# Two-layer block with a seven-product feed-forward stage: operands of successive pairs in alternating places, made one pair ahead

## What is computed

```python
h = rms_norm(x, norm2_g)
x = x + (silu(h @ w_gate) * (h @ w_up)) @ w_down      # D = 1024, F = 2816
```

## Time and profile before

| What | Value |
|---|---|
| Median of 3 runs (lowest, highest) | 2658.61 us (2657.32, 2658.63) |
| Profiled execution: its own time | 2658.09 us |
| Profiled execution: its span | 2655.9 us |
| TensorE matmul busy | 2608.4 us, 98% of the span |
| VectorE busy | 1566.0 us, 59% |
| ScalarE busy | 1131.5 us, 43% |
| GpSimd busy | 181.7 us, 7% |
| Moved by DMA | 296.76 MB, mean 112 GB/s |
| Mean granted TensorE clock, share of 2.4 GHz | 0.995 |

### The profile page before, as it was taken

One profiled execution on the slowest core, in us unless ns is written; L12 is line 12 of the kernel. 1 busy time (PEld: TensorE's weight loads), 2 busy tenths in 40 slices (PEclk: granted clock), 3 DMA queues, 4 the chain that ended last, 5 costly groups with the idle time before them and its releaser, 6 DMA issues.

```text
span 2655.9 us, 36717 instructions
## 1 busy us (share of the span) xinstructions
PE 2608.4 (98%) x15173; PEld 2181.4 (82%) x15173; DVE 1566.0 (59%) x2427; ACT 1131.5 (43%) x1714; POOL 181.7 (7%) x123
## 2 busy tenths in 40 slices
PE   9999999999999999999999999899999999989998
PEld 5788888988888879888888777798998777788997
DVE  7877767644444456543455666663763566664674
ACT  2343233533333344332343665452553465453453
POOL 0000000000000000000000110120310010020220
PEclk9999999999999999999999999999999999989999
DMA  9345754222222211232232212132233211223222
GB/s 402 129 190 209 283 197 177 90 81 79 80 80 80 75 70 67 109 103 92 94 108 106 77 64 80 64 108 92 96 109 128 82 64 64 79 80 119 80 97 86
DMA packets 46759, 296.76 MB, mean 112 GB/s; under 512 B 5121, under 2 KB 7297, under 8 KB 17410
## 3 DMA queue, kind: packets, MB, share of 16 engines
q1 hardware_dynamic: 46592, 294.42, 30.4%
q10 hardware_dynamic: 2, 0.00, 0.0%
HBM read 292.30 MB, written 2.10 MB: 111 GB/s over the span
## 4 chain that ended last, share of the span: by engine, by line
PE 85%; DVE 5%; ACT 3%; issue 3%; POOL 3%; POOLq 0%; DVEq 0%; ACTq 0%
PE PS L631 84%; POOL QV L2447 3%; ACT QH L1184 1%; PE PS L689 1%; DVE QL L1749 1%; DVE QV L1749 1%; ACT WH L1184 1%; DVE WL L1749 0%; ACT KEPT L1184 0%; DVE TV L1752 0%; DVE XT L1749 0%; DVE TV L1749 0%; DVE AA L1749 0%; DVE SId L1749 0%; POOL SId L2447 0%
## 5 line engine op out<-in xcount | busy, mean ns | idle before, releaser
L1749 DVE TENSOR_TENSOR WL<-RAW,WH 128x1024 fp32r<-128x1024 f32 (+1 forms) x328 | 429.8, 1310 | 443.4 <-ACT WH L1184 441.8
L631 PE MATMUL PS<-H1H,WH 128*128 128x512 f32 (+1 forms) x1568 | 602.6, 384 | 0.7 <-DVE H1L L1749 0.3
L631 PE MATMUL PS<-H1L,WH 128*128 128x512 f32 (+1 forms) x1568 | 590.5, 377 | 0.0
L631 PE MATMUL PS<-H1H,WL 128*128 128x512 f32 (+1 forms) x1568 | 590.4, 377 | 0.0
L1184 ACT ACTIVATE WH<-RAW 128x1024 fp32r<-128x1024 f32 (+1 forms) x328 | 365.4, 1114 | 246.0 <-PE PS L631 215.0
L631 PEld LDWEIGHTS PS<-H1H,WH 128*128 128x128 f32 x1568 | 295.2, 188 | 60.6 <-issue 5.4
L631 PEld LDWEIGHTS PS<-H1L,WH 128*128 128x128 f32 x1568 | 295.2, 188 | 56.2 <-issue 4.1
L631 PEld LDWEIGHTS PS<-H1H,WL 128*128 128x128 f32 x1568 | 295.0, 188 | 54.7
L631 PE MATMUL PS<-TH,QH 128*128 128x256 f32 x1008 | 291.7, 289 | 34.6 <-ACT KEPT L1184 22.7
L631 PE MATMUL PS<-TL,QH 128*128 128x256 f32 x1008 | 287.7, 285 | 0.0
L631 PE MATMUL PS<-TH,QL 128*128 128x256 f32 x1008 | 287.6, 285 | 0.0
(11 more groups left out here) (296 smaller groups left out, 4060.5 us busy)
## 6 DMA issues: line engine op xcount, KB each, us to landing
RAW<-stream SPq DMA_DIRECT2D x169, 1024.0 KB, 4.8
AR<-stream SPq DMA_DIRECT2D x56, 1024.0 KB, 7.2
RAW<-stream SPq DMA_DIRECT2D x64, 704.0 KB, 4.0
RT<-ret SPq DMA_DIRECT2D x2, 1536.0 KB, 6.7
MIX<-stream SPq DMA_DIRECT2D x4, 640.0 KB, 17.0
XT<-xt SPq DMA_DIRECT2D x4, 512.0 KB, 5.6
y<-XT SPq DMA_DIRECT2D x16, 128.0 KB, 1.8
MIX<-stream SPq DMA_DIRECT2D x1, 1024.0 KB, 17.0
```

What stands on the lines that cost most here:

```text
L631: return nc.tensor.matmul(out, weights, moving, start=start, stop=stop, skip_group_check=True)
L1749: return nc.vector.tensor_tensor(out, a, b, op)
```

## The change

- `STD` goes from 4 to 5: each of the two stages has five plain pairs in front, and 17 seven-product pairs instead of 18 (34 in the kernel).
- Operands lie in three places: W (where they were), H (over `H1H` and `H1L`) and G (over the part of `GHd`/`GLd` that the first seven-product pair's own output and later ones use), with a last block of G at 223232. The first pair of a stage has G, then H and W alternate. In a second half the first pair has H.
- `site(s)` replaces `product`: an operand of pair s may be written once the last pair that used the same place is through (for W also the last plain tile, for H the last plain tile in front, for G the tile before the stage).
- All operands of pair s+1 are made during pair s, on VectorE and ScalarE, in a new order. The fourth kept part moves to the head of the next pair's list on ScalarE (`last_kept`).
- The sums S2 and S4 move from GpSimd to VectorE (`second_sum`, `fourth_sum`).
- The homes of plain tiles go round by three throughout; the lists of fixed homes in the two stages are gone.
- The 19 factor steps are spread over five plain pairs.
- Semaphores `qh`, `ql` are called `qhd`, `qld`, since `qh`, `ql`, `qv` are now functions that give a block of a pair's place.

The core of the diff:

```diff
-STD = 4
+STD = 5
@@ homes
-    of, last, fixed = {}, SPLIT % 3 - 1, {}
-    for f0 in (FFN2, FFN3):
-        fixed.update(zip(range(f0 + 22, f0 + 30), (0, 1, 2, 0, 1, 0, 1, 2)))
-        fixed[f0 + 52] = 0
-    fixed.update(zip(range(FFN3, FFN3 + 2 * STD), (2, 0, 1, 2, 1, 0, 1, 2)))
...
+    plain = [t for t in range(SPLIT, NTILE) if not seven(t)]
+    return {t: (SPLIT + n) % 3 for n, t in enumerate(plain)}
+def sites():
+    out = {}
+    for f0 in (FFN2, FFN3):
+        for half in range(2):
+            for jj in range(0 if half else STD, HC):
+                first = jj == STD and not half
+                out[f0 + 30 * half + 2 * jj] = "G" if first else "H" if jj % 2 == 0 else "W"
+    return [out[t] for t in PAIRS]
@@ Core
-        self.QH, self.QL, self.QV = at("QH", 68096, 3584, F32R), at("QL", 84992, 3584, F32R), at("QV", 84992, 3584)
+        self.QH = {x: at("QH" + x, a, 3584, F32R) for x, a in (("W", 68096), ("H", 18432), ("G", 124928))}
+        self.QL = {x: at("QL" + x, a, 3072 if x == "G" else 3584, F32R)
+                   for x, a in (("W", 84992), ("H", 35072), ("G", 149504))}
+        self.QV = {x: at("QV" + x, a, 3072) for x, a in (("W", 84992), ("H", 35072), ("G", 149504))}
+        self.QLG = at("QLGA22", 223232, 512, F32R)
-    def product(self, s, name):
...
+    def site(self, s):
+        t, x = PAIRS[s], SITE[s]
+        f0 = FFN3 if t >= FFN3 else FFN2
+        pairs = [p + 1 for p, y in zip(PAIRS, SITE) if p < t and y == x]
+        if x == "W":
+            pairs.append(max(u for u in HOME if u < t))
+        return self.mm, mm_at(max(pairs[-2:] + [f0 + 2 * STD - 1 if x == "H" else f0 - 1]))
@@ act_program, seven_kept
+        if past:
+            last_kept(f, t - 2)
+        if more:
+            weights_high(s + 1)
         q.wait_ge(c.prod, 5 * s + 1)
         q.wait_ge(c.sa, 22 * (f - 2) + j)
         act(c.KEPT1[:, 0:256], E[:, 256:512]).then_inc(c.kept, 1)
-        if j % HC and seven(t - 2):
+        if past:
             gated_high(f, t0, j - 1)
         q.wait_ge(c.prod, 5 * s + 2)
         q.wait_ge(c.c2, s)
         act(c.KEPT2[:, 256:512], D[:, 256:512], scale=-1.0).then_inc(c.kept, 1)
+        if more:
+            sums_high(s + 1)
         q.wait_ge(c.prod, 5 * s + 3)
         act(c.KEPT1[:, 256:512], E[:, 256:512]).then_inc(c.kept, 1)
         if more:
-            weights_high(s + 1)
-            sums_high(s + 1)
+            second_high(s + 1)
+            rest_high(s + 1)
         else:
             prep(t + 2)
         q.wait_ge(c.sa, 22 * (f - 2) + j + 1)
         act(SI[:, :], SI[:, :], ACT.Silu).then_inc(c.si, 1)
-        if more:
-            second_high(s + 1)
-        q.wait_ge(c.mm, mm_at(t + 1))
-        act(c.KEPT2[:, 0:256], E[:, 256:512]).then_inc(c.kept, 1)
-        if more:
-            rest_high(s + 1)
-        else:
+        if not more:
+            last_kept(f, t)
             prep(t + 3)
             gated_high(f, t0, j)
@@ dve_program, seven_out
-        third_sum(s)
+        if more:
+            first_sum(s + 1)
         if past:
             gated(f, j - 1)
-        rest_low(s)
+        if more:
+            weights_low(s + 1)
+            second_sum(s + 1)
         if past:
             gated_low(f, j - 1)
         if more:
-            first_sum(s + 1)
-            weights_low(s + 1)
+            third_sum(s + 1)
+            fourth_sum(s + 1)
+            sums_low(s + 1)
+            second_low(s + 1)
+            rest_low(s + 1)
         else:
             prep(t + 2)
         q.wait_ge(c.mm, mm_at(t))
...
         tt(SI[:, :], D[:, :], c.KEPT1[:, :], ALU.subtract).then_inc(c.sa, 1)
-        if more:
-            sums_low(s + 1)
-            second_low(s + 1)
-        else:
+        if not more:
@@ dve_program, ffn
-                    factors(f, ((), (4, 5, 6, 7), (10, 11, 12), (15, 16))[jj])
+                    factors(f, ((), (4, 5, 6, 7), (10, 11), (14, 15), (18,))[jj])
...
-                    factors(f, ((0, 1, 2, 3), (8, 9), (13, 14), (17, 18))[jj])
+                    factors(f, ((0, 1, 2, 3), (8, 9), (12, 13), (16, 17), ())[jj])
@@ pool_program
-        for s in range(len(PAIRS) // 2 * l, len(PAIRS) // 2 * (l + 1)):
...
-            tt(c.QV[:, S2:S2 + 512], c.QV[:, S1:S1 + 512], raw[:, 0:512], ALU.add).then_inc(c.sum2, 1)
...
-            tt(c.QV[:, S4:S4 + 512], c.QV[:, S2:S2 + 512], raw[:, 512:1024], ALU.add).then_inc(c.sum4, 1)
```

More of the change, by code:

```diff
@@ L316, in homes @@
 def homes():
-    of, last, fixed = {}, SPLIT % 3 - 1, {}
-    for f0 in (FFN2, FFN3):
-        fixed.update(zip(range(f0 + 22, f0 + 30), (0, 1, 2, 0, 1, 0, 1, 2)))
-        fixed[f0 + 52] = 0
-    fixed.update(zip(range(FFN3, FFN3 + 2 * STD), (2, 0, 1, 2, 1, 0, 1, 2)))
[L323 to L326, removed]
+    plain = [t for t in range(SPLIT, NTILE) if not seven(t)]
+    return {t: (SPLIT + n) % 3 for n, t in enumerate(plain)}
 HOME = homes()
 COUNT = {t: n + 1 for n, t in enumerate(HOME)}
-def before(t, home):
-    return max((u for u in HOME if u < t and HOME[u] == home), default=3)
+def sites():
[6 more added lines that the diff above has]
+    return [out[t] for t in PAIRS]
+SITE = sites()
 BANK = banks()
@@ L503, in __init__ @@
         self.sum1, self.sum2, self.sum3, self.sum4 = (sem(f"sum{i}") for i in (1, 2, 3, 4))
-        self.qh, self.ql, self.prod, self.kept, self.c2 = (sem(n) for n in ("qh", "ql", "prod", "kept", "c2"))
+        self.qhd, self.qld, self.prod, self.kept, self.c2 = (sem(n) for n in ("qhd", "qld", "prod", "kept", "c2"))
     def xk(self, k):
@@ L519, in vacant, with qh, ql, qv @@
     def vacant(self, t):
[L521 to L525, removed]
-    def product(self, s, name):
[L529 to L535, removed]
+        plain = [u for u in HOME if u < t and HOME[u] == HOME[t]]
+        pairs = [p for p, x in zip(PAIRS, SITE) if p < t and x == "W"]
+        return self.mm, mm_at(max(plain[-1:] + [p + 1 for p in pairs[-1:]], default=3))
+    def site(self, s):
[5 more added lines that the diff above has]
+        return self.mm, mm_at(max(pairs[-2:] + [f0 + 2 * STD - 1 if x == "H" else f0 - 1]))
+    def qh(self, s, o, n):
+        return self.QH[SITE[s]][:, o:o + n]
+    def ql(self, s, o, n):
+        return self.QLG[:, o - A22:o - A22 + n] if SITE[s] == "G" and o >= A22 else self.QL[SITE[s]][:, o:o + n]
+    def qv(self, s, o, n):
+        return self.QV[SITE[s]][:, o:o + n]
     def pair(self, s):
@@ L1351, in seven_kept @@
         s, D, E, SI = PAIRS.index(t), PS[BANK[t]], PS[BANK[t + 1]], c.SI[f][j % HC % 2]
-        more = seven(t + 2)
+        more, past = seven(t + 2), j % HC and seven(t - 2)
+        if past:
+            last_kept(f, t - 2)
+        if more:
+            weights_high(s + 1)
         q.wait_ge(c.prod, 5 * s + 1)
@@ L1964, in first_sum, with second_sum, fourth_sum @@
         q.wait_ge(*ready)
-        q.wait_ge(*c.product(s, "S1"))
-        tt(c.QV[:, S1:S1 + 512], raw[:, 1024:1536], raw[:, 1536:2048], ALU.add).then_inc(c.sum1, 1)
+        q.wait_ge(*c.site(s))
+        tt(c.qv(s, S1, 512), raw[:, 1024:1536], raw[:, 1536:2048], ALU.add).then_inc(c.sum1, 1)
+    def second_sum(s):
+        raw = c.pair(s)[1]
+        q.wait_ge(c.sum1, s + 1)
+        tt(c.qv(s, S2, 512), c.qv(s, S1, 512), raw[:, 0:512], ALU.add).then_inc(c.sum2, 1)
+    def fourth_sum(s):
+        raw = c.pair(s)[1]
+        q.wait_ge(c.sum2, s + 1)
+        tt(c.qv(s, S4, 512), c.qv(s, S2, 512), raw[:, 512:1024], ALU.add).then_inc(c.sum4, 1)
@@ L1985, in second_low @@
     def second_low(s):
-        q.wait_ge(c.qh, 4 * s + 3)
-        q.wait_ge(*c.product(s, "A22"))
-        tt(c.QL[:, A22:A22 + 512], c.pair(s)[1][:, 1536:2048], c.QH[:, A22:A22 + 512].bitcast(F32), ALU.subtract
-           ).then_inc(c.ql, 1)
+        q.wait_ge(c.qhd, 4 * s + 3)
+        q.wait_ge(*c.site(s))
+        tt(c.ql(s, A22, 512), c.pair(s)[1][:, 1536:2048], c.qh(s, A22, 512).bitcast(F32), ALU.subtract
+           ).then_inc(c.qld, 1)
     def rest_low(s):
-        q.wait_ge(c.qh, 4 * s + 4)
+        q.wait_ge(c.qhd, 4 * s + 4)
@@ L2113, in ffn @@
                     second_low(follow)
+                    rest_low(follow)
             for n in range({0: 5, 3: 6}.get(f, 8) if half else 8):
@@ L2124, in ffn @@
                     second_low(PAIRS.index(t0 + 30))
+                    rest_low(PAIRS.index(t0 + 30))
                 if not half:
```

63 lines of the change are left out of this document (33 added, 30 removed).

## The result

The changed kernel takes 2618.25 us (median of 4 runs, 2616.72 to 2620.54), the kernel before 2658.56 us on the same chip. The ratio is 0.985, with a 95% interval of 0.9833 to 0.9867: 40.3 us less, where 41.4 were forecast. The profiled execution has a span of 2614.9 us (2655.9 before).

A forecast was written before the change was run, and what follows sets the result against it. TensorE's own pace was taken as the bound, with 34.5 us of waits listed. From 2658.1 us, -23.6 (steady waits) + 1.7 (plain pairs) - 19.5 (entries) gave 2616.7, plus 0.5 for the median: 2617 us, range 2609 to 2629.

The forecast's parts named there:

- The steady loop: Steady pairs: alternating places remove TensorE's wait of 0.66 us for a kept part in 34 waits, 23.6 us gained.
- VectorE's work: Steady pairs: with two sums more, VectorE works 9.2 of 10.06 us, so TensorE still bounds.
- about 9.8 us busy in a pair: Sign of a right forecast: VectorE's busy time in a steady pair of the changed kernel.
- 0.9 us are left: Steady pairs: VectorE's room in a period of 10.06 us, held against VectorE becoming the bound.
- VectorE becomes the bound: Rival, steady pairs: period 10.3 to 10.6 us, returning 8 to 18 us of gain, say 2630 us; chance 0.10.
- Two plain pairs: Two seven-product pairs become plain, 10.9 us each for 10.06: 1.7 us more.
- The entries: First seven-product pairs of both stages: waits shrink from 12.0 and 14.9 us to 3.9 and 3.5, gaining 19.5 us.
- TensorE is 0.4 us later against it: Second stage's entry: TensorE 0.4 us later relative to VectorE than in the first, so 3.5 us lost, not 3.9.
- I take no fall: Entries: the clock stays 1.00 behind spells of 1.35 and 2.5 us; otherwise the sum is 3.4 us higher.
- Loads and second halves: Loads land after 4.8 us, wanted 12.0 us after release; second halves' first kept part is in time: no cost.
- the late load: Rival, steady pairs: loads over 12.0 us hold a kept part, 2685 us at 14 us; chance 0.04.
- a returned wait: Rival, steady pairs: the 0.66 us wait comes back behind another instruction, only entries gain, 2641 us; chance 0.05.

The follow-up runs named there:

- experiment 1: Kernel before, with only the sums S2 and S4 moved from GpSimd to VectorE, one place kept: 2656.16 us, ratio 0.9994.
- experiment 2: Changed kernel with the sums S2 and S4 back on GpSimd: 2624.37 us, ratio 0.9873.
- experiment 5: Changed kernel with one needless 512-column VectorE instruction in each pair: 2622.68 us, ratio 0.9868.
- experiment 6: Changed kernel with two needless 512-column VectorE instructions in each pair, the second waiting for the first: 2644.03 us, ratio 0.9947.
- experiment 7: Changed kernel with one needless VectorE instruction a pair and the last kept part set ahead of SiLU on ScalarE: 2618.39 us, ratio 0.9854.
- experiment 8: Changed kernel, entry reordered: first pair's third and fourth sums, high and low parts before the fifth plain pair's gating, next high weights later: 2620.43 us, ratio 0.9859.
- experiment 10: Changed kernel run again unaltered, on one chip with a repeat of a third entry order: 2619.11 us, ratio 0.9855.
- experiment 3: Changed kernel with four plain pairs instead of five and the weights' factors spread over four: 2627.6 us, ratio 0.9886.
- experiment 4: Kernel before with five plain pairs, factors spread likewise and homes going round by three; one place and GpSimd's sums stay: 2645.15 us, ratio 0.9952.
- experiment 9: Changed kernel with a third entry order: all first-pair operands made before the fifth plain pair's gate, its SiLU and gating moved later: 2613.5 us, ratio 0.9833.
- experiment 11: Changed kernel with the third entry order (first-pair operands before the fifth plain pair's gate), repeated beside the unaltered change on one chip: 2613.99 us, ratio 0.9835.

## Why the prediction was right, and where its steps were off

**The steady loop** (forecast 23.6, measured 23.1). Confirmed by the profile, and by experiments 1 and 2 as a matter of places and not of the engine that makes the sums. The prediction did not separate the two. It took the loop from the chain of GpSimd's sum; experiment 1 shows that the loop closes also without GpSimd, through the low parts at 1895.94. Whoever had read "GpSimd is slow" from the earlier trace rows would have made half the change for nothing.

**VectorE's work** was forecast at 9.2 us a pair and measured at 9.10 busy. The line "about 9.8 us busy in a pair" under what would show it was wrong: it added durations, and the view counts an overlapped stretch once. "0.9 us are left" was the step that failed, without effect on the time. Room was taken as period less work; the hand-over from VectorE to ScalarE's SiLU and last kept part and back makes it 0.4 us (experiments 5 to 7). The rival "VectorE becomes the bound" was thus closer than its text made it: with one instruction of 512 columns more a pair, VectorE sets the period (10.28 us).

**Two plain pairs**: 1.7 forecast, 1.6 measured.

**The entries.** First stage: S1 was to wait 1.35 us and lost 1.81 (1.93 from start to start, less 0.12); S2 2.5 forecast, 2.39 lost. What was mis-sized at S1 is one low part: 1.78 us at 1710.70, and 1.22 elsewhere, beside GpSimd's product that ran from 1709.80. The Trainium skill (SBUF — State Buffer, Who interferes with whom) has it that a VectorE instruction with two SBUF inputs contends with a GpSimd instruction that reads SBUF, and the one that came first is served first. The trace agrees with its 1.78 us, and so does experiment 8: there GpSimd's product comes later, at 1712.93, and the same low part, at 1709.23, takes 1.23 us. That the contention is the cause was not tried by itself. Second stage: 3.5 us forecast, 4.23 lost. "TensorE is 0.4 us later against it" failed: the last gate instruction starts 0.97 us ahead of the first product in the first stage (1708.37, 1709.34) and 0.95 in the second (2308.04, 2308.99). The entries are alike, so the second could not be better. That the sum came within 0.4 us is in part luck: the steady pairs and the entries gave 1.6 us less than forecast, and 1.1 us came that no step of the prediction had.

**The clock at the entries** was the choice to make. In the profiled execution it stayed 1.00, as forecast, but experiment 10 shows 0.50 at the same waits in another execution, and the runs with a needless instruction fell too: of ten entries with idle spells of 1.65 and 2.23 us (the changed kernel, its repeat, experiments 5 to 7) five kept 1.00 and five fell. So "I take no fall" was right for one execution by chance. The Trainium skill's rule that activity releases the higher rate and idleness ends it (TensorE: Matmul & The Clock Gate, What's actually happening) was set aside too lightly: five of the ten entries agree with it. A fall costs 1.5 us and not the 1.7 taken. One or two of them would be enough to part the slowest run (2620.54 us, mean clock 0.998) from the profiled one (2616.72, 0.999); this is an estimate, as the other runs have no trace. The median of 2618.25 lies above the forecast by less than one fall.

**Loads and second halves** cost nothing, as forecast: no wait of TensorE stands there, and both runs of 11 pairs last 110.87 us. Of the rivals the late load did not occur, nor did a returned wait.

## What to carry to other kernels

When a wait seems to hang on a slow engine, ask first whether the place that it writes is the loop, and try the two cures one at a time: here the places (with the order that they allow) gave all of the steady gain and the faster engine none, yet the engine mattered at the entries, where nothing covers it. The idle time of an engine is not its slack. The slack is the period less the longest loop through all engines that it hands to, and a needless instruction or two measure it. Of a change in pipelines the last part of the gain lies where they fill; there the order of the lists was worth another 5 us (3.7 of wait, the rest most likely the clock).

## What was not expected of the hardware

- The same program with the same idle spells (1.66 and 2.23 us) is granted 1.00 behind them in one execution and 0.50 in the next. At the six entries whose first spell was 3.19 to 4.03 us (experiments 2 to 4, both stages) it fell to 0.50 each time, though not always behind that spell: with four plain pairs it was still 1.00 until the second spell (experiment 3, first stage). It also fell at both entries of experiment 8, with spells of 1.69, 0.40 and 2.00 us. Behind spells of 0.74 and 1.02 us (experiment 9 and its repeat) it stayed 1.00.
- Where nothing is waited for, 84 matmuls of 256 columns take 10.08 us in every pair and every run of 11 pairs 110.87, to within 0.01, in both stages and in experiments 3 and 7 to 11. A run's length is thus a finer measure than the kernel's time, in which a fall of the clock hides an effect of 1.5 us.
